# Conditioning chunks of branch B: weights as the moving operand, each chunk ahead of the wait for the exponentials

## The reference, cut to what matters

```python
mod = jnp.einsum('bd,de->be', jax.nn.silu(c), w_ada) + b_ada
sh1, sc1, gt1, sh2, sc2, gt2 = jnp.split(mod[:, None, :], 6, axis=-1)
h = rms_norm(x, g_norm1) * (1.0 + sc1) + sh1
# ... projections, branch A (sparse) and branch B (window) give merged ...
x = x + gt1 * jnp.einsum('btd,de->bte', merged, w_out)
h2 = rms_norm(x, g_norm2) * (1.0 + sc2) + sh2
u = jax.nn.relu(jnp.einsum('btd,df->btf', h2, w_up))
x = x + gt2 * jnp.einsum('btf,fd->btd', u * u, w_down)
```

## Time and profile before

| | us |
|---|---|
| median of three runs | 2016.21 |
| the three runs | 2013.92, 2016.21, 2021.88 |
| the profiled execution, device time | 2007.44 |
| its span, first to last instruction | 2005.6 |
| PE busy in the span | 1898.1 |
| DVE / ACT / POOL busy | 971.1 / 583.3 / 469.7 |
| mean granted clock of PE | 0.922 |
| branch B with chunks (765.86 to 968.98) | 203.12 |

### The profile page before, as it was taken

The page is one execution under the profiler, slowest core; times in us unless marked ns, Lnnn a source line. Parts: engine busy times, 40 slices in busy tenths (PEclk is TensorE's granted clock), DMA queues, the critical chain, the costliest instruction groups (busy, mean ns, idle before and its releaser), DMA issues.

```text
span 2005.6 us, 30234 instructions
## 1 busy us (share of the span) xinstructions
PE 1898.1 (95%) x11198; PEld 1825.6 (91%) x11198; DVE 971.1 (48%) x2232; ACT 583.3 (29%) x1115; POOL 469.7 (23%) x273
## 2 busy tenths in 40 slices
PE   7699999999989988999999968999999999999997
PEld 2598999999888888999999968999999999999996
DVE  1648888896355554322464343333334242434344
ACT  3345566631344444322231133020202020101012
POOL 0322222323111111101122313222322222322220
PEclk9699999999999897555699978999999999999998
DMA  7320233244232225332244101111111111111112
GB/s 277 113 58 24 73 97 98 87 135 127 83 98 66 59 45 157 96 107 74 67 150 156 52 21 43 43 42 42 42 42 52 42 42 42 42 43 51 42 42 89
DMA packets 179316, 153.39 MB, mean 76 GB/s; under 512 B 20240, under 2 KB 162016, under 8 KB 178688
## 3 DMA queue, kind: packets, MB, share of 16 engines
q1 hardware_dynamic: 175328, 137.31, 23.7%
q10 hardware_dynamic: 3920, 15.19, 1.9%
HBM read 127.34 MB, written 25.19 MB: 76 GB/s over the span
## 4 chain that ended last, share of the span: by engine, by line
PE 87%; DVE 5%; ACT 3%; DMA 2%; issue 2%; POOL 0%; SPq 0%; DVEq 0%; ACTq 0%; POOLq 0%
PE psum L790 63%; PE psum L1065 6%; PE psum L1083 5%; PE psum L1056 3%; PE psum L914 2%; PE psum L947 2%; PE psum L1029 2%; PE psum L1028 2%; PE psum L828 1%; DVE u_lo L1936 1%; DVE h_f L1556 1%; PE psum L1032 1%; DMA out<-y_out 1%; DVE score L1613 1%; DVE logit L1751 1%
## 5 line engine op out<-in xcount | busy, mean ns | idle before, releaser
L790 PE MATMUL psum<-h_hi,w_hi 128*128 128x362 f32 (+1 forms) x1440 | 477.9, 332 | 17.5 <-POOL h_lo L768 10.7
L790 PE MATMUL psum<-h_lo,w_hi 128*128 128x362 f32 (+1 forms) x1440 | 476.0, 331 | 0.0
L790 PE MATMUL psum<-h_hi,w_lo 128*128 128x362 f32 (+1 forms) x1440 | 475.2, 330 | 0.0
L723 POOL CAST w_hi<-w_raw 128x1024 fp32r<-128x1024 f32 x112 | 120.5, 1076 | 1059.6 <-PEq L794 861.6
L790 PEld LDWEIGHTS psum<-h_hi,w_hi 128*128 128x128 f32 x1440 | 273.2, 190 | 21.4 <-POOL h_lo L768 12.6
L725 POOL TENSOR_TENSOR w_lo<-w_raw,w_hi 128x1024 fp32r<-128x1024 f32 x112 | 275.7, 2462 | 9.0
L790 PEld LDWEIGHTS psum<-h_hi,w_lo 128*128 128x128 f32 x1440 | 273.5, 190 | 0.0
L790 PEld LDWEIGHTS psum<-h_lo,w_hi 128*128 128x128 f32 x1440 | 273.4, 190 | 0.0
L1886 DVE SCALAR_TENSOR_TENSOR xT<-psum,modT,xT 128x64 f32<-128x64 f32 (+7 forms) x288 | 136.3, 497 | 274.8 <-PE psum L790 274.8
L790 PE MATMUL psum<-u_hi,w_hi 128*128 128x362 f32 (+1 forms) x768 | 252.9, 329 | 2.7 <-DVE u_lo L1936 2.7
L790 PE MATMUL psum<-u_lo,w_hi 128*128 128x362 f32 (+1 forms) x768 | 252.1, 328 | 0.0
(11 more groups left out here) (282 smaller groups left out, 2992.4 us busy)
## 6 DMA issues: line engine op xcount, KB each, us to landing
w_raw<-in_w_in SPq DMA_DIRECT2D x32, 512.0 KB, 4.1
ada_c<-in_w_ada SPq DMA_DIRECT2D x32, 512.0 KB, 4.0
w_raw<-in_w_up SPq DMA_DIRECT2D x32, 512.0 KB, 4.0
w_raw<-in_w_down SPq DMA_DIRECT2D x32, 512.0 KB, 3.5
zT_scratch<-z_out ACTq DMA_DIRECT2D x27, 544.0 KB, 3.6
q_raw<-zT_scratch SPq DMA_DIRECT2D x32, 272.0 KB, 5.0
gate<-zT_scratch SPq DMA_DIRECT2D x16, 544.0 KB, 4.6
ada_w<-in_w_ada SPq DMA_DIRECT2D x4, 2048.0 KB, 9.4
```

The source lines that it names most:

```text
L723: pl.tensor_copy(w_hi[slot][:, :], w_raw[slot][:, :]).then_inc(sem("w_hi_made"), 1)
L790: ins = pe.matmul(bank(b, n), w[:, k, wc], x[:, a, c0:c0 + n], start=(m == 0 and p == 0), stop=(m == len(wk) - 1 and p == 2))
```

## The change

The weights become the moving operand of a chunk (128 columns a pass) and `siluT` the stationary one. A chunk's result is then two rows of 128, at columns 256 to 383 of the same bank. DVE copies these two rows into a tile `ada_rows` before it divides the unit's output: rows 32 x (j mod 4), column block j div 4; the tile is set to zero at the start of branch B. After the last outputs of branch B, PE transposes the eight blocks of `ada_rows`, and DVE adds the bias in two additions instead of four. The chunk of unit n-1 moves from `weigh_all` to the head of PE's iteration n, ahead of the wait for `probs_made` of unit n, with the wait for `y_done` in front of it. The ring has two buffers, as the third one's place is now `ada_rows`; load j waits for chunk j-2.

```diff
-        ada_c = [at(f"ada_c{s}", [P, KT, P], F32, B + (2304, 12992, 14016)[s]) for s in range(3)]
+        ada_c = [at(f"ada_c{s}", [P, KT, P], F32, B + (2304, 12992)[s]) for s in range(2)]
+        ada_rows = at("ada_rows", [P, 8, P], F32, B + 14016)
...
-        def ada_bank(j):
-
-            return bank(6 + (NA + j) % 2)
+        def ada_out_at(j):
+
+            return bank(6 + (NA + j) % 2, 512, slice(0, 2))[:, 2 * P:3 * P]
...
-                if j >= 3:
-                    sp.wait_ge(sem("ada_used"), 4 + j - 2)
-                sp.dma_start(ada_c[j % 3][:, :, :],
+                if j >= 2:
+                    sp.wait_ge(sem("ada_used"), 4 + j - 1)
+                sp.dma_start(ada_c[j % 2][:, :, :],
...
-                pe.wait_ge(sem(f"ada_c_in{j % 3}"), 16 * (j // 3 + 1))
+                pe.wait_ge(sem(f"ada_c_in{j % 2}"), 16 * (j // 2 + 1))
                 for k in range(KT):
-                    ins = pe.matmul(ada_bank(j)[:, 256 + 2 * j:258 + 2 * j], ada_c[j % 3][:, k, :], siluT[:, k::KT],
+                    ins = pe.matmul(ada_out_at(j), siluT[:, k::KT], ada_c[j % 2][:, k, :],
                                     start=(k == 0), stop=(k == KT - 1))
                 ins.then_inc(sem("ada_used"), 1)
...
-                if 0 <= u["n"] - NA < NADA:
-                    ada_chunk(u["n"] - NA)
                 for k, (g, before, tiles) in enumerate(groups):
...
                 n = u["n"]
+                if 0 <= n - 1 - NA < NADA:
+                    pe.wait_ge(sem("y_done"), n - 2)
+                    ada_chunk(n - 1 - NA)
                 pe.wait_ge(sem("probs_made"), n + 1)
...
                 turn_outputs(7, part)
+            for m in range(8):
+                ins = pe.transpose(bank(6, 1024)[:, m * P:m * P + P], ada_rows[:, m, :], ident[:, :])
+            ins.then_inc(sem("ada_turned"), 1)
...
-            def mod_out(c0, n, ps, step=1):
+            def mod_out(c0, n, by_s):
 
                 for s in range(2):
-                    ins = dv.tensor_tensor(modT[:, c0:c0 + n:step, s], ps.rearrange("p (m s) -> p m s", s=2)[:, ::step, s],
-                                           vecT[:, c0:c0 + n:step], ALU.add)
-                    link(ins)
+                    link(dv.tensor_tensor(modT[:, c0:c0 + n, s], by_s[s], vecT[:, c0:c0 + n], ALU.add))
...
                 dv.wait_ge(sem(f"probT_used{g % 2}"), before + 1)
+                j = n - NA
+                if 0 <= j < NADA:
+                    dv.tensor_copy(ada_rows[32 * (j % 4):32 * (j % 4) + 2, j // 4, :], ada_out_at(j))
                 if u["blk"] is None:
...
+                    link(dv.memset(ada_rows[:, :, :], 0.0))
                     dv.wait_ge(sem("biasB_in"), 16)
...
-            dv.wait_ge(sem("ada_used"), 4 + NADA)
-            for odd in range(2):
-                mod_out(16 + odd, NADA - odd, ada_bank(odd)[:, 256 + 2 * odd:256 + 2 * NADA], step=2)
+            dv.wait_ge(sem("ada_turned"), 1)
+            mod_out(16, NADA, [bank(6, 1024)[:, s::32] for s in range(2)])
```

More of the change, by code:

```diff
@@ L641, in load_ada_chunk @@
             def load_ada_chunk(j):
-                if j >= 3:
-                    sp.wait_ge(sem("ada_used"), 4 + j - 2)
-                sp.dma_start(ada_c[j % 3][:, :, :],
+                if j >= 2:
+                    sp.wait_ge(sem("ada_used"), 4 + j - 1)
+                sp.dma_start(ada_c[j % 2][:, :, :],
                              bass.AP(w_ada.tensor, 2 * DM + P * j, [[6 * DM, P], [P * 6 * DM, KT], [1, P]]))\
-                    .then_inc(sem(f"ada_c_in{j % 3}"), 16)
+                    .then_inc(sem(f"ada_c_in{j % 2}"), 16)
             def load_mix_w(i, u):
@@ L1545, in _ @@
             dv.wait_ge(sem("mod_turned"), 1)
-            mod_out(0, 16, bank(6, 32))
+            mod_out(0, 16, [bank(6, 32)[:, s::2] for s in range(2)])
             gain(gain1, 1, 48)
```

## The result

| | before | after |
|---|---|---|
| median of the runs, us | 2015.07 | 1930.09 |
| lowest to highest, us | 2011.38 to 2021.88 | 1928.07 to 1936.47 |
| profiled execution, device time, us | 2007.44 | 1928.07 |
| its span, us | 2005.6 | 1926.3 |
| mean granted clock | 0.922 | 0.972 |

The ratio is 0.958, 95% interval 0.9545 to 0.9615. The forecast was 1935 us in a range of 1920 to 1990.

A forecast was written before the change was run, and what follows sets the result against it. PE at the low clock bounds branch B, half of it the chunk. Terms -80 (stretch) + 1.1 (memset) - 2.5 (tail) + 0.5 (transposes) = -81 us, off the 2016.2 us median: 1935 us, range 1920 to 1990.

The forecast's parts named there:

- The clock follows the streams: Branch B: chunks of loads let the clock fall, chunks of streams hold it up; 203.1 us becomes 113.7 at 1.00.
- The rule weighed against it: Branch B: by the skill's page, a chunk keeping PE as busy as before changes no clock; 2019 us.
- rival 2: Branch B: the clock does not follow the streams; chunk 3.4 instead of 3.2 us, 2019 us, no change; chance 0.09.
- A pass of 128 columns, 0.107 us: Turned chunk in branch B: a pass takes 0.107 us if its load hides, otherwise 0.12; chunk 1.71 us.
- The count of 114.4 us: Branch B stretch at full clock: passes 54.8, values 27.4, turns 12.8, logits 15.4, outputs 4.0 us; up to 121.
- Falling clock (5 us allowed) and stalls (2 us allowed): Branch B stretch: 5 us (0 to 20) for the clock falling again, 2 us (0 to 6) for stalls.
- The query split: Odd head of each pair in branch B: ready at 8.9 us, wanted at 9.3; 0 to 2 us for each pair.
- The place: Chunk ahead of the exponentials' wait covers six DVE-copy waits (3.8 us), no further gain; failed cover returns 5.4 us.
- Rival 2's price: No-change sum for branch B: chunks add 6 us, memset and transposes 2, six covered stalls give back 5.4: 2019 us.
- The ring of two: Chunk loads in branch B: landing 4.0 us against 5.3 available; fits with 1.3 us to spare, except slow loads.
- Memset and copies: Branch B: memset at its start, 1.1 us on the path (0.5 to 1.1); 32 DVE copies, 7 us, beside PE.
- The tail: End of branch B, 12.63 us: clock saves 2.5 us (0 to 5), new transposes add 0.5 (0 to 1.0).

The follow-up runs named there:

- the two parts alone: Changed kernel with the chunk left beside the values: 1949.8 us, ratio 0.9607; kernel before with its old chunk ahead of the wait for exponentials: 2012.21 us, ratio 0.9924.
- the cut kernels: Kernel before and changed kernel, each with one of the eight products of each chunk: 1935.75 us (ratio 0.9544) and 1935.85 us (ratio 0.9544).
- the place alone: Kernel before with its old chunk moved ahead of the wait for the exponentials, ring of three, no copies: 2012.21 us, ratio 0.9924.

## Why the prediction was right, step by step

- **The clock follows the streams.** Right: 0.99 over the stretch, and the two parts alone tell it from the place (0.94 for the turned chunk, 0.53 for the place). The reason I gave was half right. I wrote that a chunk of loads lets the clock fall; the cut kernels show that it falls without most of those loads too. And two rows that I read as signs of it had gaps in them. In the transposes of the prologue PE was busy for 18.75 of 35 us, after an idle time of 4.60 us; and the clock fell in branch B at 779.9 us, behind a microsecond in which PE was busy for 0.30:

```profile
778.00:779.00 1.00, 0.30 (x2) 0.14 (x1) 0.80 (x3) 0.00 (x0) 0.00 (x0) 1.00 0.47 130
779.00:780.00 1.00, 0.96 (x8) 0.99 (x9) 0.85 (x6) 0.12 (x1) 0.00 (x0) 0.94 0.96 288
```

  Those rows fit the streams and the gaps alike; what parts the two is the place alone.
- **The rule weighed against it.** The Trainium skill, "TensorE: Matmul & The Clock Gate", section "Why this matters for your kernels", on keeping TensorE busy without gaps: the runs agree with one half and not with the other. A gap did drop the clock (2.80 us idle, then 3.20 us a chunk). Being busy did not hold it (200.72 of 201.50 us at 0.53). What the prediction calls the third case beside this rule is its rival 2, no change.
- **A pass of 128 columns, 0.107 us.** It took 1.84/16 = 0.115, inside the bounds (0.107 to 0.12): 32 x 0.13 = 4.2 us more than the sum had. The 56 ns that the Trainium skill, "TensorE: Matmul & The Clock Gate", section "Back-to-back issue gap", gives for an isolated pass is out for these float32 operands, and so are the 81 ns that the section gives for passes with their loads.
- **The count of 114.4 us.** Two terms that I took from rows before moved with the new order. The turn rose from 0.44 to 0.59 us, since its loads no longer start under the step ahead: about 30 x 0.15 = 4.5 us that I had missed. The values fell from 0.96 to 0.85 us: 2.8 less.
- **Falling clock (5 us allowed) and stalls (2 us allowed).** The clock did not fall again; only the first chunk ran at 1.2 GHz, 3.23 us, 1.4 us more (1.7 forecast). The stalls were larger: PE was idle for 129.87 - 123.01 = 6.9 us. The query split came as worked out, up to 0.8 us in each of three pairs, 2.4 in all. What I had not seen was the way from values over copy, bias, exponentials, high and low part back to the next outputs: 4.0 us of waits in the stretch, 5.1 with the tail. The two errors cancel, 5 us too much and 4.9 too little, and that is luck. What is left between the 123 us forecast and the 129.87 measured is the passes, the turns and the values above (5.9 us); about 1 us stays open.
- **The place.** I wrote that the new place covers the waits for copies and gave it no further gain; if the cover failed, 5.4 us were to come back. With the turned chunk beside the values 12 us came back: 5.0 us of waits for copies, 6.0 us more of waits for POOL (less the waits for low parts, which went), and the low clock. In that stretch PE was idle for 13.4 instead of 6.5 us and busy for 128.53 instead of 120.85. The sum had the waits as covered, so the forecast did not suffer; the price of the failing cover was too small.
- **Rival 2's price.** It took 5.4 us off for covered waits at the low clock. The place alone showed that a longer chunk and a longer turn (32 x 0.2 = 6.7 us) eat them up.
- **The ring of two.** Right: landing 4.1 us (3.7 to 6.9), one wait of 0.3 us. It becomes a bound of 2 to 3 us once the other waits are taken away.
- **Memset and copies.** 0.92 us and its wait of 0.16, on the path, as worked out (1.1). A copy takes 0.282 us instead of 0.22, off the path.
- **The tail.** 4.2 us gained, where 2.0 net was forecast. The clock stayed at 1.00; the transposes took 1.02 us in place of PE's wait:

```profile
901.35 0.24 PE psum L1077
901.59 1.02 PE psum L1147 x8
902.62 2.52 PE psum L791 x14
```

  Part of this is luck. In one of the two other profiled executions of the same kernel the clock fell in the tail, as the prediction had feared, and the tail took 9.36 us instead of 8.39:

```profile
906.44 1.90 PE psum L1147 x8
```

- **The time that came out.** The forecast took 81 us off. By the trace the change is worth 73.3 + 4.2 - 1.2 = 76.3 us: the stretch gained less than forecast, the tail more. The medians moved by 85.0 us, 8.7 more: 3.0 lie in the rest of the two profiled executions (branch B's earlier start above all), and 5.6 come from the profiled execution of before, which lies 7.6 us under its median, where that of after lies 2.0 under. So 1930 instead of 1935 us does not mean that the change did better than forecast.

## What to carry to other kernels

When PE is fully busy and its clock row is low, look for what it is busy with. Here two operand orders of the same product cost nearly the same at equal clock (1.68 and 1.84 us a chunk), and yet a unit took 6.70 us with one and 3.75 with the other: passes of 128 moving columns came with a clock of 0.99, loads of 128 columns with two-column products with 0.53 to 0.56. Work that streams can be nearly free in such a mix, so before taking it out ask at which clock the rest would run. Once the stage was at the high clock, the waits of 2.8 us were paid twice, so a filler belongs ahead of the step that waits; waits of up to 0.8 us were not.

## What the runs showed of the hardware that was not expected

- Leaving out 51 us of passes shortened the stretch by 4.5 us, and the clock went from 0.99 to 0.67.
- One idle time of 2.80 us was followed by a chunk of 3.20 instead of 1.84 us; with the chunk beside the values a spell of low clock came behind each of the three such waits, in all three executions profiled.
- Behind a turned chunk (two stationary columns) the 128-column loads of the next step come about 0.2 us late, with no engine that PE waited for: ahead of the turn (32 times, 7.1 us in all) or, at the old place, ahead of the values (32 times, 7.8 us). Behind the old chunk (128 stationary columns) with the same waits they start in time. The cause stays open.
